# Two of three gate/up pairs of the feed-forward up stages by seven half-width products

## The reference

```python
D_MODEL = 1024; SEQ = 512; D_FF = 2816
u = rms_norm(h, norm_ffn_g[l])
g, up = jnp.split(u @ w_gate_up[l], 2, axis=-1)
h = h + (jax.nn.silu(g) * up) @ w_down[l]
...
h = rmsnorm(x, g_ffn_pre[l])
gu = h @ w_ffn_in[l]
f = (jax.nn.silu(gu[..., :D_FF_2]) * gu[..., D_FF_2:]) @ w_ffn_out[l]
```

## Time and profile before

| | us |
|---|---|
| median of three runs | 1701.86 (1701.81 to 1701.96) |
| span of the profiled execution, first to last instruction | 1699.9 |
| what lies around the span (median less span) | 1.96 |
| TensorE busy | 1690.9 (99%) |
| VectorE, ScalarE, GpSimd busy | 883.4, 656.4, 682.4 |

### The profile page before, as it was taken

How to read it: one execution, slowest core, us unless ns; L and a number is a source line. 1 busy time by engine, 2 the same in 40 slices (tenths; PEclk the granted TensorE clock), 3 DMA queues, 4 the chain that set the end, 5 groups by cost and what they waited for, 6 DMA issues and landing times.

```text
span 1699.9 us, 23574 instructions
## 1 busy us (share of the span) xinstructions
PE 1690.9 (99%) x8081; PEld 1359.4 (80%) x8085; DVE 883.4 (52%) x1406; ACT 656.4 (39%) x1091; POOL 682.4 (40%) x308
## 2 busy tenths in 40 slices
PE   9999999999999999999999999999999999999998
PEld 7888767788888888888788766678888988888887
...
PEclk9999999999999999999999999999999999999999
...
GB/s 202 115 152 152 102 63 51 75 87 124 99 99 98 90 97 99 99 98 138 128 88 87 50 38 51 51 74 90 96 99 99 88 99 92 94 98 99 99 97 65
DMA packets 47635, 162.29 MB, mean 95 GB/s; under 512 B 5724, under 2 KB 7900, under 8 KB 47304
## 3 DMA queue, kind: packets, MB, share of 16 engines
...
## 4 chain that ended last, share of the span: by engine, by line
PE 52%; issue 32%; POOL 12%; ACT 1%; DVE 1%; DMA 1%; POOLq 0%; SPq 0%; ACTq 0%; DVEq 0%
PE ps L527 14%; PE ps L529 14%; PE ps L528 14%; POOL w_lo L443 12%; PE ps L1153 1%; PE ps L1152 1%; PE ps L1151 1%; PE ps L708 1%; PE ps L726 1%; PE ps L752 1%; PE ps L1052 1%; PE ps L1011 1%; PE ps L1033 1%; PE ps L980 1%; DMA hT<-xT 0%
## 5 line engine op out<-in xcount | busy, mean ns | idle before, releaser
L443 POOL TENSOR_TENSOR w_lo<-w_raw,w_hi 128x1024 fp32r<-128x1024 f32 x260 | 643.2, 2476 | 892.8 <-ACT w_hi L1234 866.1
L527 PE MATMUL ps<-u_hi,w_hi 128*128 128x512 f32 x1336 | 540.0, 404 | 0.2 <-ACTq L1824 0.2
L529 PE MATMUL ps<-u_hi,w_lo 128*128 128x512 f32 x1336 | 521.7, 390 | 0.0
L528 PE MATMUL ps<-u_lo,w_hi 128*128 128x512 f32 x1336 | 521.3, 390 | 0.0
L1234 ACT ACTIVATE w_hi<-w_raw 128x1024 fp32r<-128x1024 f32 x271 | 285.5, 1055 | 391.9 <-PE ps L529 326.4
L527 PEld LDWEIGHTS ps<-u_hi,w_hi 128*128 128x128 f32 x1336 | 251.2, 188 | 58.5 <-issue 8.6
L529 PEld LDWEIGHTS ps<-u_hi,w_lo 128*128 128x128 f32 x1336 | 250.9, 188 | 53.0
L528 PEld LDWEIGHTS ps<-u_lo,w_hi 128*128 128x128 f32 x1336 | 251.4, 188 | 51.1 <-issue 1.4
L1657 ACT ACTIVATE tmp<-tmp 128x512 f32<-128x512 f32 x44 | 27.8, 632 | 213.2 <-DVEq L2339 213.2
L2349 DVE TENSOR_TENSOR a_lo<-tmp,a_hi 128x512 f32 (+1 forms) x44 | 104.2, 2368 | 4.7
L527 PE MATMUL ps<-a_hi,w_hi 128*128 (+1 forms) x264 | 103.0, 390 | 0.0
...
## 6 DMA issues: line engine op xcount, KB each, us to landing
...
```

The source lines that it names most:

```text
L443: pool.tensor_tensor(w_lo[:, slot], w_raw[:, slot], w_hi[:, slot].bitcast(F32), ALU.subtract)\
L527: pe.matmul(out, wh, xh, start=start, stop=False)
L528: pe.matmul(out, wh, xl, start=False, stop=False)
L529: return pe.matmul(out, wl, xh, start=False, stop=stop)
```

## The change

Of every three gate/up pairs two are no longer formed by 2 x 24 products of 512 columns. Gate tile a and up tile b are each cut into two halves of the contraction (a0, a1, b0, b1), and the input into two halves of the contraction and two halves of the tokens (L the first 256 tokens, H the last). Seven products of halves, each 4 blocks x 3 = 12 products of 256 columns, take the place of the eight that the plain way has: a0·u0L, a1·u1L, b1·t4, (a0-b0)·t3, (b0+b1-a0)·t2, (b0+b1)·t1 and (a0+a1-b0-b1)·u1H. Here t1 to t4 are differences of the input's halves, made once per stage (`t_sums`, t_hi, t_lo). The three weight sums are made for each such pair: VectorE adds in float32 (`weight_sums`, s_raw, and b0+b1 in place in w_raw), ScalarE rounds them (`sums_hi`, s_hi, 128 x 1536), GpSimd subtracts (`sums_low`, s_lo, 128 x 1536). The parts are put together by `copy` on ScalarE and by `late_sums`, `late_up` and `fast_gate` on VectorE. Loop turns of six units (two such pairs, one plain pair) cover 36 of the 44 units in the first up stage and 30 in the second; the other units stay plain. Activations are kept unsplit (a_raw); ScalarE rounds and VectorE subtracts all 22 at the stage's end (`split`), and the down stage waits for them two at a time.

```diff
+        a_raw = ar("a_raw", [P, FT, T], F32, 44)
+        HALF = T // 2
+        HK = KT // 2
+        t_hi = ar("t_hi", [P, HK, 4, HALF], F32R, 0)
+        t_lo = ar("t_lo", [P, HK, 4, HALF], F32R, 16)
+        s_raw = ar("s_raw", [P, 3, T], F32, 32)
+        s_hi = [ar("s_hi0", [P, 3, T], F32R, 38), at("s_hi1", [P, 3, T], F32R, mk_at)]
+        s_lo = [ar("s_lo0", [P, 3, T], F32R, 88), ar("s_lo1", [P, 3, T], F32R, 94)]
+        t_raw = [ar(f"t_raw{i}", [P, 4, HALF], F32, 80 + 4 * i) for i in range(2)]
...
+        FAST = {"ffn1": (FIRST["ffn1"] + 2 * R, 6), "ffn2": (FIRST["ffn2"] + 4 * R, 5)}
+        E_BANK = 3
...
+                        if j in (0, 2):
+                            sp.wait_ge(*summed)
...
+            def sums_low(name, i, pair):
+                n = i * 2 + (pair % 3 + 2 * (pair // 3) + 1)
+                pool.wait_ge(*of_fast(name, "s_hi", n))
+                pool.wait_ge(*of_fast(name, "s_used", n))
+                pool.tensor_tensor(s_lo[pair % 3][:, :, :], s_raw[:, :, :], s_hi[pair % 3][:, :, :].bitcast(F32),
+                                   ALU.subtract).then_inc(named("raw_lo"), 1)
...
+                def turn(i, last):
+                    low(i, u + 2)
+                    sums_low(name, i, 1)
+                    for j in (3, 4, 5, 6):
+                        low(i, u + j)
+                    if not last:
+                        sums_low(name, i, 3)
+                    low(i, u + 7)
...
+            def half_product(out, w_h, w_l, x_h, x_l, start, stop):
+                for k in range(HK):
+                    pe.matmul(out, w_h(k), x_h(k), start=start and k == 0, stop=False, skip_group_check=True)
+                    pe.matmul(out, w_h(k), x_l(k), start=False, stop=False, skip_group_check=True)
+                    m = pe.matmul(out, w_l(k), x_h(k), start=False, stop=stop and k == HK - 1, skip_group_check=True)
...
+                prod = named("fast_prod")
+                pe.wait_ge(lo_ready, t + 1)
+                acquire(x)
+                half_product(ps[:, x, L], *natural(a, 0), *of_u(0, L), True, False)
+                pe.wait_ge(*of_fast(name, "s_lo", i * 2 + (e + 1)))
+                half_product(ps[:, x, H], *summed(1), *of_t(2), False, True).then_inc(prod, 1)
+                acquire(y)
+                half_product(ps[:, y, L], *summed(0), *of_t(1), True, False)
+                pe.wait_ge(lo_ready, t + 2)
+                half_product(ps[:, y, H], *natural(b, 0), *of_t(0), False, True).then_inc(prod, 1)
+                pe.wait_ge(*of_fast(name, "copied", i * 2 + (e + 1)))
+                half_product(ps[:, x, L], *natural(a, 1), *of_u(1, L), False, True).then_inc(w_used, 1)
+                half_product(ps[:, x, H], *natural(b, 1), *of_t(3), False, True).then_inc(w_used, 1)
+                pe.wait_ge(*of_fast(name, "z", i * 2 + (e + 2)))
+                half_product(ps[:, y, H], *summed(2), *of_u(1, H), False, True).then_inc(named("fast_s_used"), 1)
...
+                with repeat(pe, turns, [(uses[b], 1) for b in (0, 1, 4, 5, 6, 7)]) as i:
+                    for e in range(2):
+                        seven_products(name, i, e, u + 2 * e)
+                    for j in (4, 5):
+                        tile_unit(i * (2 * R) + (u + j), (u + j) % R, ffn2_banks(2)[j % 2], u_hi, u_lo)
...
-                    pe.wait_ge(made, FT - 2)
+                    pe.wait_ge(*of_fast(made, "a_lo", 2))
...
+                def t_tile(k):
+                    act.wait_ge(*of_fast(name, "t_raw", k + 1))
+                    act.activation(t_hi[:, k], t_raw[k % 2][:, :, :], ACT.Copy).then_inc(named("raw_hi"), 1)
...
+                def sums_hi(i, pair):
+                    summed(i, pair)
+                    act.wait_ge(*of_fast(name, "s_used", i * 2 + (pair % 3 + 2 * (pair // 3) + 1)))
+                    act.activation(s_hi[pair % 3][:, :, :], s_raw[:, :, :], ACT.Copy).then_inc(named("raw_hi"), 1)
+                def copy(i, e):
+                    act.wait_ge(*of_fast(name, "prod", i * 4 + (2 * e + 1)))
+                    act.wait_ge(*of_fast(name, "z", i * 2 + (e + 1)))
+                    act.activation(first_two[:, :], ps[:, ffn2_banks(e)[0], :], ACT.Copy)\
+                       .then_inc(named("fast_copied"), 1)
+                def split(k):
+                    act.wait_ge(*of_fast(name, "a", k + 1))
+                    act.activation(a_hi[:, k], a_raw[:, k], ACT.Copy).then_inc(named("raw_hi"), 1)
+                def turn(i, last):
+                    feed_at(i, 2)
+                    copy(i, 0)
+                    sums_hi(i, 1)
+                    feed_at(i, 3)
+                    feed_at(i, 4)
+                    gate(ps[:, E_BANK, :])
+                    copy(i, 1)
+                    feed_at(i, 5)
+                    feed_at(i, 6)
+                    gate(ps[:, E_BANK, :])
+                    if last:
+                        act.wait_ge(*of_fast(name, "s_used", 2 * turns + 2))
+                        if at_end:
+                            at_end()
+                        for k in range(4):
+                            split(k)
+                        feed_at(i, 7)
+                        plain_gate()
+                        for k in range(4, 8):
+                            split(k)
+                        feed_at(i, 8)
+                        for k in range(8, 12):
+                            split(k)
+                        feed_at(i, 9)
+                        plain_gate()
+                        for k in range(12, 20):
+                            split(k)
+                    else:
+                        sums_hi(i, 3)
+                        feed_at(i, 7)
+                        plain_gate()
...
-                    a = tmp[4][:, :].unsqueeze(1)
-                    step(dve.tensor_scalar(a_hi[:, bass.ds(k, 1)], a, 1.0, None, ALU.mult))
-                    step(dve.tensor_tensor(a_lo[:, bass.ds(k, 1)], a, a_hi[:, bass.ds(k, 1)].bitcast(F32), ALU.subtract))
-                    dve.sem_inc(named(name + "_a"), 1)
...
+                def t_sums(k):
+                    col, late = v(gain, k), v(gain, HK + k)
+                    b11 = late_two[:, L]
+                    if k >= 2:
+                        dve.wait_ge(*of_fast(name, "t_hi", k - 1))
+                    t1, t2, t3, t4 = [t_raw[k % 2][:, n] for n in range(4)]
+                    step(dve.tensor_scalar(b11, hT[:, k, L], col, None, ALU.mult))
+                    step(dve.scalar_tensor_tensor(out=t1, in0=hT[:, k, H], scalar=col, in1=b11,
+                                                  op0=ALU.mult, op1=ALU.subtract))
+                    step(dve.scalar_tensor_tensor(out=t2, in0=hT[:, HK + k, H], scalar=late, in1=t1,
+                                                  op0=ALU.mult, op1=ALU.subtract))
+                    step(dve.tensor_tensor(t3, t2, b11, ALU.subtract))
+                    step(dve.scalar_tensor_tensor(out=t4, in0=hT[:, HK + k, L], scalar=late, in1=t2,
+                                                  op0=ALU.mult, op1=ALU.subtract))
+                    dve.sem_inc(named("fast_sum"), 1)
+                def t_low(k):
+                    dve.wait_ge(*of_fast(name, "t_hi", k + 1))
+                    step(dve.tensor_tensor(t_lo[:, k], t_raw[k % 2][:, :, :], t_hi[:, k].bitcast(F32), ALU.subtract))
+                    dve.sem_inc(named("raw_lo"), 1)
...
+                def weight_sums(i, pair):
+                    c = u + 2 * pair
+                    a, b = c % R, (c + 1) % R
+                    for t in (c, c + 1):
+                        dve.wait_ge(landed[t % R], i * 32 + (16 * (t // R) + 16))
+                    dve.wait_ge(*of_fast(name, "s_lo", i * 2 + (pair % 3 + 2 * (pair // 3))))
+                    step(dve.tensor_tensor(s_raw[:, 1], w_raw[:, a, 0:T], w_raw[:, b, 0:T], ALU.subtract))
+                    step(dve.tensor_tensor(w_raw[:, b, 0:T], w_raw[:, b, 0:T], w_raw[:, b, T:2 * T], ALU.add))
+                    step(dve.tensor_tensor(s_raw[:, 0], w_raw[:, b, 0:T], w_raw[:, a, 0:T], ALU.subtract))
+                    step(dve.tensor_tensor(s_raw[:, 2], w_raw[:, a, T:2 * T], s_raw[:, 0], ALU.subtract))
+                    dve.sem_inc(named("fast_sum"), 1)
+                def late_sums(i, e):
+                    dve.wait_ge(*of_fast(name, "prod", i * 4 + (2 * e + 2)))
+                    dve.wait_ge(*of_fast(name, "copied", i * 2 + (e + 1)))
+                    step(dve.tensor_tensor(late_two[:, :], ps[:, ffn2_banks(e)[1], :], first_two[:, :], ALU.add))
+                    dve.sem_inc(named("fast_z"), 1)
+                def late_up():
+                    step(dve.tensor_tensor(late_two[:, H], late_two[:, H], late_two[:, L], ALU.add))
+                def fast_gate(i, e):
+                    x, y = ffn2_banks(e)
+                    dve.wait_ge(*of_fast(name, "s_used", i * 2 + (e + 3)))
+                    step(dve.tensor_tensor(tmp[1][:, H], ps[:, y, H], late_two[:, L], ALU.add))
```

(35 more changed lines are left out.)

312 lines of the change are left out of this document (219 added, 93 removed).

## The result

The changed kernel takes 1761.16 us (median, 1760.80 to 1761.68) against 1701.91 of the kernel before on the same chip: ratio 1.0346, interval 1.0332 to 1.0361. It is slower, as forecast, and by more: 59.5 us between the profiled spans (1759.4 against 1699.9) where the sum had 41.8, and just outside the range of 1696 to 1757.

The account below looks back on a forecast made before the run. It took TensorE, busy 99% of a 1699.9 us span, as the bound. Terms -18.2 + 40.5 + 5.6 + 0.9 + 8.2 + 3.1 + 1.7 = +41.8 gave 1743 us predicted, range 1696 to 1757.

Parts of the forecast that it names:

- TensorE, -18.2: Up stages: 84 steps of 256 columns replace 48 of 512, saving 0.83 us per pair, 18.2 us over 22 pairs.
- The exclusion: VectorE instructions reading SBUF twice and GpSimd instructions exclude each other; together they take 30.3 of a turn's 31 us.
- The chain of a turn, 34.67: Loop turn: dependent steps across engines take 34.67 us where TensorE needs 30.99; eleven turns lose 40.5 us.
- The two terms around the turn of VectorE's loop (0.87 + 1.94): Turn's chain: `plain_up` with its increments 0.87 us, then the first of the next four sums, behind a low part, 1.94.
- a first sum of some 2 us: Sign to look for: the first of VectorE's four weight sums takes some 2 us.
- GpSimd's low part, 3.51: GpSimd's subtraction of 128 x 1536 takes 3.51 us, extrapolated from smaller sizes, with bounds 3.0 and 3.7.
- The start, first stage: First up stage: TensorE loses 5.6 us before the first p1 and 0.9 us for a unit fed late.
- The start, second stage: Second up stage: 8.2 us lost ahead of unit 11, and 3.1 us more for the first sums' low part.
- the 3.1 us for the first sums' low part: Second up stage's start: the low part of the first weight sums costs 3.1 us more.
- The end: "hidden": Stage ends: the splits run hidden behind TensorE's work; holds delay one ring unit, 0.84 us in each stage.
- Rival A: Loop turns: the exclusion falls into gaps and TensorE stays the bound, turns of 30.99 us; 1689.7 us, chance 0.18.
- Rival B: Whole kernel: turns bound by TensorE but the starts' losses stand; +1.3 us, 1703 us, chance 0.05.

Follow-up runs that it names:

- E4: Changed kernel with weight sums, their high and low parts formed over 64 of 512 columns, their products reading activations as weights: 1713.86 us, measured once.
- E2: Changed kernel with one input of three kinds of VectorE gate multiplications in PSUM instead of SBUF: 1736.21 us.
- E8: Changed kernel with ScalarE's feeds of units 11 and 12 moved earlier at the second stage's start: 1760.00 us.
- E1: Changed kernel with ScalarE's squares of the memory norm placed behind the first feeds of down1a instead of ahead of them: 1748.97 us.
- E10: E9 with only one of a turn's three pairs by seven half-width products, the other two by whole width: 1697.12 us, ratio 0.9969 to the kernel before.
- E11: E10 with E2's part undone, so three kinds of VectorE multiplications again have two SBUF inputs: 1700.81 us.
- E5: Changed kernel with E1's and E2's edits together, and PSUM bank 2 given back after the last fast turn: 1719.53 us.
- E9: E5 with half-width turns begun six units later in both stages, five and four turns instead of six and five: 1703.86 us.

## Why the prediction was right in direction and wrong in size

- **TensorE, -18.2.** Right: steps of 0.12 us at full clock, and E4's turn of 31.06 against 30.99. The seven fulfilled waits of a pair cost nearly nothing.
- **The exclusion.** Right, and now shown and not only read: E2 changes nothing but the memory of one input, and takes the means from 1458, 1927 and 1870 ns to those of free instructions. The Trainium skill, "GPSIMD Engine Reference", section 8 (Key points), puts it on the shared SBUF interfaces; by that rule, E2 agrees. One reading was too narrow: the class isn't only instructions that read SBUF twice. L2348 of the earlier trace rows reads one tensor and was held as well (1.22 in place of 0.43), and in the changed kernel one L2601 (256 columns of one tensor) took 2.49 us from 407.69 in place of 0.35, beside GpSimd's w_lo of 2.66 from 407.37.
- **The chain of a turn, 34.67.** Right within 0.45 us: 35.12, with the waits at p6 (2.1) and at p1 of the second pair (1.3) as forecast. Term by term, from 496.15 to 531.27 in the changed kernel: from p1 to `fast_gate` 8.94 us instead of 8.62, and ScalarE's two roundings 1.65 instead of 1.54 each; the rest cancels to within 0.1. The two terms around the turn of VectorE's loop (0.87 + 1.94) are right in sum, 2.82, but by another make-up: the first weight sum took 0.95 us and was hardly held, and VectorE idled 0.67 and 0.50 us ahead of L2583 and L2631. So of the signs "a first sum of some 2 us" did not come; L2655 at 2.28 us in every second call did. All eleven turns together lost about 43 us where the sum had 40.5.
- **GpSimd's low part, 3.51.** Right: 3.50. The Trainium skill's "GPSIMD Engine Reference", section 2.1 (Instruction dispatch), with its 2.5 cycles a column, gave the estimate of 3.2 us; here that is too low, and the measurement decides.
- **The start, first stage.** p1's wait right (5.4 of 5.6 us); the unit fed late waited 2.9 us, not 0.9; the slow clock behind p1's wait (14 steps in 3.08 us) took 1.4 that no term had.
- **The start, second stage.** Unit 11's wait right (8.5 of 8.2). The clock behind it (some 3 us) was missed, and the 3.1 us for the first sums' low part weren't lost: TensorE's own delay covered them. The two nearly cancel. E8 shows that the mechanism is VectorE's chain and not the feed's place.
- **The end: "hidden".** This is the step that failed. It compared rates: two of 22 splits per 5.44 us are more than VectorE needs. That holds for TensorE, which never waits for a split. But I followed only who waits for the splits' results, not what is queued behind them: L2194 of the memory norm stands behind twelve splits on VectorE, L1417 waits for it on ScalarE, and three weight feeds stand behind L1417. With 0.8 forecast and 12.3 lost (9.8 of waiting, 2.4 of slow clock behind it), it is 11.5 of the 17.7 us of error; E1 takes nearly all of it away (12.2 us) by changing ScalarE's order alone. The other 6 us are sizes: some 3 in the turns, 2.0 at the unit fed late, 1.4 of slow clock.
- **Rival A** (the holds fall into gaps) failed for two pairs a turn and is true for one: E10 and E11 have turns bound by TensorE. **Rival B**'s state (TensorE-bound turns, the starts standing) is E4 at 1713.9, with the end's 12 us in it that B did not have.

Where the time went, by what gives it back in this order of edits: 12.2 us the queue at the end (E1), 29.4 the holds of three kinds of multiplication in turns and starts (E5), 15.7 the starts (E9). E9 is still 1.7 us above the kernel before: 1.5 us are lost before unit 5, and the nine turns save 0.08 us each in place of 1.65, since the 1.3 us wait for s_lo before the second p1, with the slower steps around it, eats the rest. Whether s_lo could come earlier in GpSimd's queue wasn't tried.
